# Merged two-sided retrieval instructions, gate sums in ScalarE's exponential, and a mixing product with tokens innermost, in a decoder layer with product-key experts

## What is computed

```python
q = (xt @ w_q).reshape(n_tok, 8, 2, 128)
s = jnp.einsum('nhcd,hckd->nhck', q, sub_keys)          # two key sides c, 128 keys each
s1, i1 = lax.top_k(s[:, :, 0], 16)
s2, i2 = lax.top_k(s[:, :, 1], 16)
cand_s = (s1[..., :, None] + s2[..., None, :]).reshape(n_tok, 8, 256)
cand_i = (i1[..., :, None] * 128 + i2[..., None, :]).reshape(n_tok, 8, 256)
top_s, pos = lax.top_k(cand_s, 16)
experts = jnp.take_along_axis(cand_i, pos, axis=-1)
gates = jax.nn.softmax(top_s, axis=-1)
h = gelu(einsum('td,thed->the', x, u_tab[experts]))
y = einsum('the,thed->td', gates * h, v_tab[experts])
out = layer_norm(ALPHA * x + y)
```

## Time and profile before

| | us |
|---|---|
| median of three runs | 1572.98 |
| the profiled execution | 1584.14 |
| its span, first to last instruction | 1582.4 |
| TensorE busy | 1454.7 |
| VectorE busy | 1257.0 |
| ScalarE busy | 963.6 |
| GpSimd busy (issuing gathers) | 704.4 |

### The profile page before, as it was taken

The page is one execution under the profiler, slowest core; times in us unless marked ns, Lnnn a source line. Parts: engine busy times, 40 slices in busy tenths (PEclk is TensorE's granted clock), DMA queues, the critical chain, the costliest instruction groups (busy, mean ns, idle before and its releaser), DMA issues.

```text
span 1582.4 us, 26748 instructions
## 1 busy us (share of the span) xinstructions
PE 1454.7 (92%) x10262; PEld 1325.8 (84%) x10262; DVE 1257.0 (79%) x2221; ACT 963.6 (61%) x1576; POOL 704.4 (45%) x461
## 2 busy tenths in 40 slices
PE   9999999999999979998999897988999999889974
PEld 8999899988889878887888786878879989889962
DVE  5689999866795699988999797989976566556687
ACT  5433344553256557786878677676777566556683
POOL 0000110100023236776766534644478868657781
PEclk9999999999999989999999998998898999999998
DMA  7574553366499999999999999999999999999993
GB/s 261 176 250 178 193 179 142 134 259 249 171 421 426 425 424 417 416 417 416 393 392 417 402 348 384 381 393 403 409 404 369 416 417 415 414 413 407 416 382 141
DMA packets 85200, 540.82 MB, mean 342 GB/s; under 512 B 25622, under 2 KB 26294, under 8 KB 29366
## 3 DMA queue, kind: packets, MB, share of 16 engines
q0 software_dynamic: 63520, 401.96, 62.9%
q1 hardware_dynamic: 20884, 137.00, 22.9%
q10 hardware_dynamic: 672, 0.21, 0.1%
HBM read 682.45 MB, written 4.19 MB: 434 GB/s over the span
## 4 chain that ended last, share of the span: by engine, by line
DMA 29%; DVE 12%; PE 10%; issue 5%; ACT 3%; POOL 3%; POOLq 0%; DVEq 0%; ACTq 0%
DMA uv_row<-in_uv_tab,turned 29%; DVE uv_row L1875 7%; PE psum L917 5%; POOL uv_row L539 3%; ACT uv_row L1330 2%; PE psum L1033 2%; PE psum L991 2%; DVE first_key L1926 0%; PE psum L1020 0%; ACT L1297 0%; DVE psum L2059 0%; DVE x L1956 0%; DVE stats L1947 0%; DVE y_last L1885 0%; PE psum L980 0%
## 5 line engine op out<-in xcount | busy, mean ns | idle before, releaser
L539 POOL DMA_INDIRECT uv_row<-in_uv_tab,turned x388 | 607.3, 1565 | 346.9 <-PE psum L917 199.7
L1330 ACT ACTIVATE uv_row<-uv_row,turned 128x1024 f32<-128x1024 f32 x448 | 472.8, 1102 | 164.0 <-DMA uv_row<-in_uv_tab,turned 148.5
L1875 DVE CUSTOM_DVE_ANT_0 uv_row<-uv_row,x 128x2048 f32<-128x2048 f32 x144 | 330.1, 2292 | 83.3 <-DMA uv_row<-in_uv_tab,turned 54.5
L1875 DVE CUSTOM_DVE_ANT_0 uv_row<-uv_row,x_mirrored 128x2048 f32<-128x2048 f32 x112 | 256.9, 2294 | 93.5 <-DMA uv_row<-in_uv_tab,turned 87.2
L917 PE MATMUL psum<-scratch,uv_row 128*128 128x128 f32 x1312 | 168.2, 280 | 30.4 <-ACT uv_row L1330 30.0
L917 PEld LDWEIGHTS psum<-scratch,uv_row 128*128 128x128 f32 x1312 | 148.0, 143 | 48.6 <-ACT uv_row L1330 45.5
L605 PE MATMUL psum<-xT_hi,w_hi 128*128 128x256 f32 x640 | 183.9, 287 | 3.1 <-DVE w_lo L1451 2.6
L1033 PE MATMUL psum<-scratch,dense_unit 128*128 128x128 f32 x1536 | 185.0, 276 | 0.0
L606 PE MATMUL psum<-xT_lo,w_hi 128*128 128x256 f32 x640 | 181.7, 284 | 0.0
L607 PE MATMUL psum<-xT_hi,w_lo 128*128 128x256 f32 x640 | 181.7, 284 | 0.0
L991 PE MATMUL psum<-x1T,dense_unit 128*128 128x256 f32 x768 | 180.3, 382 | 0.0
(11 more groups left out here) (302 smaller groups left out, 2082.6 us busy)
## 6 DMA issues: line engine op xcount, KB each, us to landing
w_raw<-in_w_stream SPq DMA_DIRECT2D x63, 1024.0 KB, 4.8
dense_unit<-in_dense_u SPq DMA_DIRECT2D x24, 1024.0 KB
dense_unit<-in_uv_tab SPq DMA_DIRECT2D x24, 1024.0 KB
wq_first<-in_w_stream SPq DMA_DIRECT2D x8, 1024.0 KB, 11.9
uv_row<-in_uv_tab,turned POOLq DMA_INDIRECT x388
wq_third<-in_w_stream SPq DMA_DIRECT2D x4, 1024.0 KB
xT_raw<-in_xT SPq DMA_DIRECT2D x4, 512.0 KB, 6.3
turned_rows<-dist_row POOLq DMA_DIRECT2D x1, 2048.0 KB
```

Of the source, the lines that this page charges most:

```text
L539: pool.indirect_dma_start(dst, None, tab, bass.IndirectOffsetOnAxis(ap=ids, axis=0), bounds_check=tab.shape[0] - 1, oob_is_err=False).then ...
L1330: act.activation(v, v, ACT.Identity, scale=w).then_inc(scaled, 1)
L1875: dve.tensor_tensor_reduce(row[k][:, 0:D], row[k][:, 0:D], x_row, 1.0, 0.0, ALU.mult, ALU.add, dots[:, s:s + 1]).then_inc(dots_done, 1)
```

## The change

Four things. The tiles for indices, positions and keys of the two sides lie side by side in one tile each (they did so in memory before), so that `hits` and `experts` work on both sides with one instruction: one conversion of 32 columns in place of two of 16 (twice), one comparison, one product and one sum over 512 columns in place of two over 256. `gates_in` no longer subtracts: it writes minus the best sum, and ScalarE's exponential takes it as its bias. The exponential also gives the sum of its results (accum_out), so the sum in `gates_out` goes. `chunk_mix` walks `mixed` keys outside, tokens innermost, where before it was tokens outside, keys innermost; the product in PSUM is read with a step of 24 instead of one after the other.

```diff
--- before.py
+++ after.py
@@ -259,16 +259,20 @@
         key_flat = tmp("peer", TI * 2 * PH * PK)
         key_sc = key_flat.rearrange("p (i u k) -> p i u k", i=TI, u=2 * PH)
 
-        val, idxf, posf = ([sb(f"{n}{c}", [P, TOP]) for c in range(2)] for n in ("val", "idxf", "posf"))
+        val = [sb(f"val{c}", [P, TOP]) for c in range(2)]
+        idxf_both, posf_both = (sb(n, [P, 2 * TOP]) for n in ("idxf", "posf"))
+        idxf, posf = ([t[:, c * TOP:(c + 1) * TOP] for c in range(2)] for t in (idxf_both, posf_both))
         of_dense = sb("of_dense", [P, TOP])
         dense_key = sb("dense_key", [P, DENSE])
         dense_key_i = sb("dense_key_i", [P, RANKED_KEYS], U32)
         dense_count = sb("dense_count", [P, RANKED_KEYS])
-        idx, posp = ([sb(f"{n}{c}", [P, TOP], U32) for c in range(2)] for n in ("idx", "posp"))
+        idx_both, posp_both = (sb(n, [P, 2 * TOP], U32) for n in ("idx", "posp"))
+        idx, posp = ([t[:, c * TOP:(c + 1) * TOP] for c in range(2)] for t in (idx_both, posp_both))
         pos = sb("pos", [P, TOP], U32)
         cand_both = tmp("peer", 2 * TOP * TOP)
         cand = [cand_both[:, c * TOP * TOP:(c + 1) * TOP * TOP] for c in range(2)]
-        hit = [t.rearrange("p (r j) -> p r j", j=TOP) for t in cand]
+        hit = cand_both.rearrange("p (r j) -> p r j", j=TOP)
+        hit_sides = cand_both.rearrange("p (c r j) -> p c r j", c=2, j=TOP)
         gate = sb("gate", [P, TI, SLOTS])
         gsum = sb("gsum", [P, PH])
         ginv = sb("ginv", [P, PH])
@@ -311,7 +315,8 @@
         iota_wide_i = at_early("iota_wide_i", [P, PK], 3072, I32)
         slot_key = [cand[0], cand[1], qc]
         back = [back_first[:, :], cand_both]
-        key_of = [at_early(f"key_of{c}", [P, TI, SLOTS], 4096 + 1024 * c) for c in range(2)]
+        key_both = at_early("key_of", [P, 2, TI, SLOTS], 4096)
+        key_of = [key_both[:, c, :, :] for c in range(2)]
         y_last = at_early("y_last", [P, 512], 4096)
         row_gate = at_early("row_gate", [P, TI, SLOTS], 6144)
         popular = at_early("popular", [P, PK], 7168)
@@ -1294,7 +1299,7 @@
                 i, h = RANKED[r]
                 act.wait_ge(gate_sub, r + 1)
                 g = gate[:, i, h * TOP:(h + 1) * TOP]
-                act.activation(g, g, ACT.Exp).then_inc(gate_exp, 1)
+                act.activation(g, g, ACT.Exp, bias=gsum[:, h:h + 1], accum_out=ginv[:, h:h + 1]).then_inc(gate_exp, 1)
 
             def gelu(s):
 
@@ -1765,27 +1770,20 @@
 
                 dve.tensor_scalar(posp[0][:, :], pos[:, :], 4, None, ALU.logical_shift_right)
                 dve.tensor_scalar(posp[1][:, :], pos[:, :], TOP - 1, None, ALU.bitwise_and)
-                for c in range(2):
-                    last = dve.tensor_copy(idxf[c][:, :], idx[c][:, :])
-                link(last)
-                for c in range(2):
-                    last = dve.tensor_copy(posf[c][:, :], posp[c][:, :])
-                link(last)
-                for c in range(2):
-                    last = dve.tensor_tensor(hit[c], across(posf[c][:, :]), iota_v, ALU.is_equal)
-                link(last)
+                link(dve.tensor_copy(idxf_both[:, :], idx_both[:, :]))
+                link(dve.tensor_copy(posf_both[:, :], posp_both[:, :]))
+                both = [P, 2 * TOP, TOP]
+                link(dve.tensor_tensor(hit, posf_both[:, :].rearrange("p (r o) -> p r o", o=1).to_broadcast(both),
+                                       iota_f[:, 0:TOP].rearrange("p (o j) -> p o j", o=1).to_broadcast(both), ALU.is_equal))
 
             def experts(r):
 
                 i, h = RANKED[r]
                 q = i * PH + h
                 pick = [t[:, i, h * TOP:(h + 1) * TOP] for t in key_of]
-                for c in range(2):
-                    last = dve.tensor_tensor(hit[c], hit[c], down(idxf[c][:, :]), ALU.mult)
-                link(last)
-                for c in range(2):
-                    last = dve.tensor_reduce(pick[c], hit[c], AX.X, ALU.add)
-                link(last)
+                link(dve.tensor_tensor(hit_sides, hit_sides, idxf_both[:, :].rearrange("p (c o j) -> p c o j", c=2, o=1).to_broadcast([P, 2, TOP, TOP]),
+                                       ALU.mult))
+                link(dve.tensor_reduce(key_both[:, :, i, h * TOP:(h + 1) * TOP], hit_sides, AX.X, ALU.add))
                 if (i, h) in BEFORE:
                     j = 1 if r == 0 else 0
                     dve.scalar_tensor_tensor(out=eid[:, q * TOP + j:(q + 1) * TOP], in0=pick[0][:, j:], scalar=float(PK),
@@ -1843,16 +1841,14 @@
 
                 i, h = RANKED[r]
                 g = gate[:, i, h * TOP:(h + 1) * TOP]
-                link(dve.tensor_copy(gsum[:, h:h + 1], g[:, 0:1]))
-                dve.tensor_scalar(g, g, gsum[:, h:h + 1], None, ALU.subtract).then_inc(gate_sub, 1)
+                dve.tensor_scalar(gsum[:, h:h + 1], g[:, 0:1], -1.0, None, ALU.mult).then_inc(gate_sub, 1)
 
             def gates_out(r):
 
                 i, h = RANKED[r]
                 g = gate[:, i, h * TOP:(h + 1) * TOP]
                 dve.wait_ge(gate_exp, r + 1)
-                link(dve.tensor_reduce(gsum[:, h:h + 1], g, AX.X, ALU.add))
-                link(dve.reciprocal(ginv[:, h:h + 1], gsum[:, h:h + 1]))
+                link(dve.reciprocal(ginv[:, h:h + 1], ginv[:, h:h + 1]))
                 link(dve.tensor_scalar(g, g, ginv[:, h:h + 1], None, ALU.mult))
                 if r == 0:
                     link(dve.tensor_copy(row_gate[:, i, h * TOP:(h + 1) * TOP], g))
@@ -1938,8 +1934,8 @@
             def chunk_mix(c):
 
                 dve.wait_ge(chunk_done, c + 1)
-                w = mixed[:, :, c * CHUNK:(c + 1) * CHUNK].rearrange("p j t -> p t j")
-                dve.tensor_tensor(w, w, chunk_bank(c)[:, 0:CHUNK * DENSE].rearrange("p (t j) -> p t j", j=DENSE),
+                w = mixed[:, :, c * CHUNK:(c + 1) * CHUNK]
+                dve.tensor_tensor(w, w, chunk_bank(c)[:, 0:CHUNK * DENSE].rearrange("p (t j) -> p j t", j=DENSE),
                                   ALU.mult).then_inc(chunk_mixed, 1)
 
             def row_stats(i, n):
```

## The result

The changed kernel takes 1577.73 us, the median of 13 runs (1575.48 to 1584.42), beside 1574.27 us of the kernel before (13 runs, 1570.49 to 1579.44). The ratio is 1.0024, 95% interval 1.0012 to 1.0035. The forecast was 1566.0 us, the range 1557 to 1576. So the time is within 0.5% of before, and not faster at all. One execution of a kernel used further down, p_mix, took 7435.61 us and has no part in its ratio.

The account below looks back on a forecast made before the run. The prediction took bytes to set the pace over most of the expert stage, with VectorE full in some stretches; 0.4 + 2.9 + 3.6 = 6.9 us off the median 1573.0 gave 1566.0 us, range 1557 to 1576.

Parts of the forecast that it names:

- (a): Mixing product: the stepped PSUM read costs as much as SBUF's steps did; 3.3 us saved, 1569.7 us, chance 0.20.
- (c): Mixing product: the stepped PSUM read costs more than both old steps; 1587 us at 2.0 us each, chance 0.07.
- ScalarE's added work: Gates: reading the accumulator adds 3.0 us to ScalarE over 16 exponentials, beside other work; price 3.0 us if uncovered.
- 600 to 760 us stayed at 416 GB/s: Retrieval stretch where bytes set the pace; nothing saved, and its getting shorter would prove the forecast wrong.
- What of it lies on the path: Whole kernel: of VectorE's saved time, 0.4 + 2.9 + 3.6 = 6.9 us shorten the end.
- The larger term: From 980 to 1200 us: 60% of the mixing products' 6.0 us counts, 3.6 us.
- 416 GB/s as the rate that the queues can have everywhere: Expert stage: stretches below this gather rate lost time, 28 us in all, winnable without fewer bytes.
- full, therefore the path: VectorE at 760 to 820, 890 to 920 and 980 to 1200 us: its saved time counts, 2.9 and 3.6 us.
- The smaller term: Retrieval at 760 to 820 and 890 to 920 us: VectorE full for 3.1 groups at 0.93 us, 2.9 us saved.
- rival (d): Whole kernel: VectorE's time is saved but the end does not move, only the start is won; 1572.6 us, chance 0.08.
- The 0.4 us at the start: First rank's retrieval, which the first gathers wait for, is 0.4 us shorter, so all behind starts 0.4 us earlier.
- The forecast's test of itself: From 980 to 1200 us: wrong if the rate stays at 394 GB/s with a mixing product of 0.55 us.

Follow-up runs that it names:

- p_mix: Kernel before with only the mixing product changed to walk tokens innermost; 1577.65 us, ratio 1.0019.
- less_dve: Kernel before with one-hot keys built for the first two chunks only, 33 us less of VectorE expected; 1574.36 us, ratio 0.9990.
- less_pe: Kernel before with each chunk's 16 products of 24 columns made one of 384, less TensorE work; 1575.63 us, ratio 0.9999.
- c_after: The changed kernel, timed and profiled a second time; 1578.49 us, ratio 1.0019.
- dose_dve: Kernel before with each rank's comparison pair on VectorE done twice; 1576.29 us, ratio 1.0005.
- dose_dve5: Kernel before with each rank's comparison pair on VectorE done five times; 1597.26 us, ratio 1.0137.
- g_bias: Kernel before with only minus the best sum as the exponential's bias, VectorE still summing; 1577.15 us, ratio 1.0013.
- g_sum: Kernel before with only the gates' sum moved to ScalarE's exponential, the subtraction left on VectorE; 1578.05 us, ratio 1.0010.

## Why the prediction was wrong

What held: the cost of each edit. The retrieval, the gates and the mixing product saved 20.9 us by their groups, 18.5 us by the page's busy time, where 21 had been worked out, the stepped PSUM read is free (rivals (a) and (c) fall with 0.549 us), ScalarE's added work is hidden, and 600 to 760 us stayed at 416 GB/s.

The step that failed is "What of it lies on the path": that VectorE is full from 760 to 820, 890 to 920 and 980 to 1200 us and that its saved time is the path's there, 2.9 + 3.6 us of the 6.9. The larger term, 3.6 us from 980 to 1200, measured nothing: slots 114 to 168 take 202.9 and 202.5 us in the two profiles of the changed kernel and 200.8 and 200.9 in those of before, and 29 us less of VectorE there did not shorten them. The step rests on two readings. The first took 416 GB/s as the rate that the queues can have everywhere and booked everything below as lost to an engine. But the DMA share in these stretches was 0.98 and 0.99, next to full, and less_dve and less_pe show that the rate of 397 or 398 GB/s between these slots stays when either engine has some 30 us to spare. Why the rate is lower there was not tried. The second took a busy share of 90 to 95% as "full, therefore the path". An engine that has just enough to do between one row and the next is as busy, and its waits (17.1 us in 220) look like little, but they are slack: the 6 us went into them nearly one for one.

The smaller term, 2.9 us in the retrieval, is not refuted as clearly. From the first dot to slot 105 the changed kernel takes 505.3 and 506.4 us (after, c_after), the kernel before and its copy 508.5 and 508.1, and dose_dve, with 12 us more, 508.4; all parts and doses but dose_dve5 lie from 507.3 to 508.6. The stretch of 60 us that starts 319 us behind the first dot has 397 and 395 GB/s with the change, 385 and 390 without. So some 2 to 3 us were probably won by slot 105. At slot 168 nothing of it is left that can be told: 746.2 and 748.6 us from the first dot, beside 748.6 and 748.2. A lead was gained and did not last through the next stage, where the forecast added the terms up as if it would.

So rival (d) was nearest, which had 0.08: the engine's time is saved and the end does not move. The 0.4 us at the start can't be seen in profiles whose first dots lie up to 6.6 us apart. That the change came out at 1.0024 and not below 1 is not explained by any part; an unchanged copy stands at 1.0007. Of the 11.7 us between the forecast and the measured median 1.3 us are the kernel before, which had 1572.98 us in three runs and 1574.27 in thirteen.

The forecast's test of itself was right: it named a rate that stays at 394 with a product of 0.55 us as the sign of its failure, and that is what the profile after shows.

## What to carry to other kernels

Before a saving on a busy engine is counted, add the same amount of work to it, in the same place: 12 us more on VectorE in the retrieval and 13.6 us on ScalarE cost nothing that could be told here, and the first of these already said that the saving in the retrieval would bring little. Look at the DMA's busy share before a lower rate is called lost: at 0.98 with 398 GB/s some 30 us less of either engine won nothing here, at 0.90 with 350 GB/s VectorE was the pace-maker. A saving off the path is not lost for good: with 11.5 MB fewer bytes the same edit brought 7.5 us, so it belongs with the next cut of bytes. And where a difference is under 0.3%, time an unchanged copy beside it.

## What the runs showed of the hardware

Walking PSUM with a step of 24 floats costs VectorE nothing that shows (0.549 us for 384 columns, beside 0.552 for the unstepped product in SBUF), while the step of 1 KB through SBUF, read and written, had cost 0.38 us. The Trainium skill (SBUF — State Buffer, "Specifications (TRN2)") gives SBUF lines of 16 bytes with a penalty for each cross to a new line, and PSUM lines of 8 bytes. The forecast read the penalty as one of PSUM too; for a VectorE operand of float32 this case shows none. A bias from a tile in place of none made ScalarE's exponential of 16 columns 0.09 us longer, 216 to 308 ns (g_bias); the accumulated output adds an instruction of 186 ns behind it and leaves the exponential itself at 216 ns where there is no bias (g_sum).
